# ScalarE's order inside a step of causal attention: copies of turned probabilities before the new tile's exponentials

## The chip, the core and the metric

The program runs on one core of a Trainium2 chip. The metric is the time of one execution on the device, in microseconds, as the median of several runs; lower is better. TensorE (PE) multiplies and transposes, VectorE (DVE) and ScalarE (ACT) read its results out of the eight PSUM banks, GpSimd (POOL) and SyncE (SP) mostly issue DMAs.

## The reference

One inference step of a two-layer trunk: layer 0 mixes tokens by a gated short convolution, layer 1 by multi-head latent attention, and each is followed by a gated convolutional FFN (width 1024, hidden 2816). It is applied to a prompt of 1024 tokens and to 8 sequences with one new token each. The change lies in the prompt's attention:

```python
s = (jnp.einsum('bthc,bsc->bhts', q_lat, kv_lat, preferred_element_type=jnp.float32)
     + jnp.einsum('bthr,bsr->bhts', q_pe, k_pe, preferred_element_type=jnp.float32)) * ATTN_SCALE
mask = k_pos[None, :] <= q_pos[:, None]
s = jnp.where(mask[None, None], s, jnp.finfo(jnp.float32).min)
p = jax.nn.softmax(s, axis=-1).astype(kv_lat.dtype)
return jnp.einsum('bhts,bsc->bthc', p, kv_lat)
```

There are 8 heads. The kernel computes it per head with expanded keys (128 wide, plus 64 rotated) and expanded values (128 wide), which is the same function.

## The kernel before

Each engine has its own instruction stream, written out by hand; semaphores order them. The weights of every layer pass through TensorE in stages (short convolution, FFN 0, the projections of layer 1, the prompt's attention, the attention of the 8 sequences over their paged cache, FFN 1). The prompt's attention takes from about 1520 us to 1766 us of the profiled span and stands between two of these stages.

The attention works on 64 units: 8 heads by 8 tiles of 128 query rows. Unit n belongs to head n // 8, and its tile is `ORD[n % 8]` with `ORD = [7, 0, 6, 1, 5, 2, 4, 3]`, so a large tile and a small one alternate. Tile i attends to i + 1 blocks of 128 keys. A tile of 4 or more has its scores in two PSUM banks (two such pairs exist), a smaller one in bank 4 (there is one). The chain of one unit n is:

1. TensorE, `scores(n)` (L2286 to L2291). A small tile waits for the exponentials of unit n-2 (`e_ready` of n-1), which free bank 4; a large one for those of unit n-4.
2. VectorE, `top(n)` (L1765): the row maxima.
3. ScalarE, `exp(n)` (L1170): exponentials out of PSUM into `p_small` or `p_big`, with row sums.
4. VectorE, `norm(n)` (L1770, L1773): reciprocal and scaling.
5. TensorE, `turn(n)` (L1861, the helper of all transposes): the probabilities are transposed block by block in items of up to four blocks; items alternate between banks 5 and 6, so item a waits until item a-2 has been copied out.
6. ScalarE, `turned_out(n)` (L1181): the copy of each item into `p_t`. From the second head on it also waits until all `values` of the head before are done, since they read `p_t`.
7. TensorE, `values(n)` (L2313): after units 2, 3, 6 and 7 of a head, the product of values and turned probabilities into bank 7 (8, 6, 4 and 2 products for units 2, 6, 7 and 3; the trace counts each twice). It waits for the copies of unit n and until bank 7 is free.
8. ScalarE, `values_out(n)` (L1191): bank 7 into `oh`, from where SyncE's DMAs (L649) carry it to memory.

Steps run over n. In step n TensorE does `scores(n)`, `turn(n-3)`, `values(n-4)`; VectorE does `top(n)`, then `norm(n-1)`; ScalarE does `exp(n)`, `values_out(n-5)`, `turned_out(n-3)` in the kernel before. The program's last four or five steps have no `scores` and no `exp`.

Of the kernel before, what the change touches and what calls it, by code (L numbers as in the profile page):

```python
# [127 lines left out]
def build(nc, ins, outs):  # L128
# [205 lines left out]
    with ExitStack() as ctx:  # L334
        ps = ctx.enter_context(nc.psum_tensor("ps", [P, 8, 512], F32))

        def bank(b):
            return ps[:, b, :]
# [62 lines left out]
        UNITS = H * KT_TOK  # L401
        PV_AFTER = {2: 3, 3: 0, 6: 2, 7: 1}

        def q_tile(n):
            return ORD[n % KT_TOK]

        def turn_items(n):

            return sum(q_tile(u) // 4 + 1 for u in range(n))

        def values_before(n):

            return sum(u % KT_TOK in PV_AFTER for u in range(n))

        def score_ps(n):
            if q_tile(n) >= 4:
                b = 2 * (n // 2 % 2)
                return ps[:, b:b + 2, :].rearrange("p b n -> p (b n)")[:, 0:(q_tile(n) + 1) * P]
            return bank(4)[:, 0:(q_tile(n) + 1) * P]

        def p_sb(n):
            return (p_big if q_tile(n) >= 4 else p_small)[n // 2 % 3]
# [406 lines left out]
        def _(act):  # L829
# [335 lines left out]
            def exp(n):  # L1165
                nk = (q_tile(n) + 1) * P
                act.wait_ge(nm_ready, n + 1)
                if n >= 6:
                    act.wait_ge(p_t_mm, turn_items(n - 5))
                act.activation(p_sb(n)[:, 0:nk], score_ps(n), ACT.Exp, bias=st[:, 0, n % 4:n % 4 + 1],  # L1170
                               accum_out=st[:, 1, n % 4:n % 4 + 1]).then_inc(e_ready, 1)

            def turned_out(n):
                i = q_tile(n)
                if n >= KT_TOK:
                    act.wait_ge(pv_mm, values_before(n // KT_TOK * KT_TOK))
                for item in range(i // 4 + 1):
                    k0, k1 = 4 * item, min(4 * item + 4, i + 1)
                    a = turn_items(n) + item
                    act.wait_ge(p_t_mm, a + 1)  # L1180
                    act.activation(p_t[i // 2][:, k0:k1, (i % 2) * P:(i % 2 + 1) * P],  # L1181
                                   bank(5 + a % 2)[:, 0:(k1 - k0) * P].rearrange("p (k n) -> p k n", n=P),
                                   ACT.Copy).then_inc(p_t_e, 1)

            def values_out(n):
                if n >= 0 and n % KT_TOK in PV_AFTER:
                    j = values_before(n)
                    act.wait_ge(pv_mm, j + 1)
                    if j >= 2:
                        act.wait_ge(head_out[j % 2], 16 * heads_out(j))  # L1190
                    act.activation(oh[j % 2][:], bank(7)[:, 0:256], ACT.Copy).then_inc(pv_e, 1)  # L1191

            for n in range(UNITS + 5):
                if n < UNITS:
                    exp(n)
                values_out(n - 5)
                if 3 <= n < UNITS + 3:
                    turned_out(n - 3)

            act.wait_ge(head_out[0], 48 * H)  # L1200
            act.wait_ge(head_out[1], 48 * H)
# [41 lines left out]
        def _(dve):  # L1243
# [257 lines left out]
            def down22(d, t0):  # L1501
# [46 lines left out]
                if more:  # L1548
                    for m in range(1, KD):
                        add_x(j0 + 2, m, sqx)  # L1550
                    lo_to(i0 + 5)
                    inv_root(q_post(d, 2) + 1)
                    rs_in(q_post(d, 2) + 1)
                    x_stored(d, 2)
                    modulate(j0 + 2, xc, xc, A, B)
                    h_low(j0 + 2, xc, B, range(KD))
                else:
                    for _, n in y_tiles(2):
                        y_out_tile(yt, n)
                        yt += 1  # L1560
# [911 lines left out]
```

## Time and profile before

| | |
|---|---|
| median of 3 runs | 2880.59 us (2876.94 to 2887.14) |
| the profiled execution | 2884.39 us, its span 2882.6 us |
| TensorE, matmuls and transposes | 2691.8 us busy, 93% of the span |
| VectorE | 1199.4 us, 42% |
| ScalarE | 860.0 us, 30% |
| mean granted clock of TensorE | 0.964 |

TensorE is busy nearly all the time, so the stretches in which it isn't are what an order of work can change. One head of the attention, from the first product of its first scores to that of the next head's, lasts about 30.3 us. Within a head the profile can be read step by step with the list above: the line tells the part of the chain, the shape tells the tile.

### The profile page before, as it was taken

Reading aid. Unit: us, or ns where it says so; the run is one execution under the profiler, and the core shown is the slowest. Engines: PE = TensorE matmul, PEld = TensorE weight load, DVE = VectorE, ACT = ScalarE, POOL = GpSimd, SP = SyncE. Lnnn points to the kernel's source line nnn. Section 1 sums busy time; section 2 is a strip of 40 time slices with the busy share of each in tenths; the row PEclk is TensorE's granted clock in tenths of the full one; section 3 lists DMA queues with packets and bytes.
Section 4 is the critical chain, followed back from the end, with each engine's and each line's share of the span. In section 5 each row is a group of like instructions: output and inputs, shape, how many; then the busy total and the mean of one; then the engine's idle time right before and its main releaser. Section 6 shows DMA issues by size and latency. Waiting matters only on the chain.

```text
span 2882.6 us, 39971 instructions
## 1 busy us (share of the span) xinstructions
PE 2691.8 (93%) x17488; PEld 2498.7 (87%) x17488; DVE 1199.4 (42%) x1849; ACT 860.0 (30%) x1359; POOL 123.7 (4%) x183
## 2 busy tenths in 40 slices
PE   5899999899999999997998888987989999999997
PEld 3888999899999999997946666657989999999997
DVE  3522237533333346653443333434743333334553
ACT  3211124222121234432333434423422222214342
POOL 1000000000000000000010000200000000000000
PEclk7999999899999999998999999987989999999998
DMA  9565223121121156542100123624312112116653
GB/s 344 217 233 200 79 99 109 59 66 60 59 72 59 59 185 202 184 134 80 30 16 14 35 110 137 272 95 145 123 52 70 61 59 66 59 61 198 201 169 117
DMA packets 320847, 330.71 MB, mean 115 GB/s; under 512 B 14349, under 2 KB 297330, under 8 KB 310877
## 3 DMA queue, kind: packets, MB, share of 16 engines
q1 hardware_dynamic: 299089, 205.48, 22.8%
q0 software_dynamic: 21584, 122.67, 11.1%
q8 instruction: 138, 2.26, 0.3%
q14 instruction: 36, 0.29, 0.0%
HBM read 282.85 MB, written 45.48 MB: 114 GB/s over the span
## 4 chain that ended last, share of the span: by engine, by line
PE 84%; DVE 8%; DMA 3%; ACT 3%; issue 2%; POOL 0%; DVEq 0%; ACTq 0%; SPq 0%; POOLq 0%
PE ps L1992 15%; PE ps L1994 15%; PE ps L1993 15%; PE ps L2027 7%; PE ps L2029 6%; PE ps L2028 6%; PE ps L1861 4%; PE ps L2313 2%; PE ps L2286 2%; PE ps L1870 1%; DVE ss_x L1343 1%; DVE o_sb L1403 1%; DVE xc L1408 1%; PE ps L1908 1%; PE ps L2377 1%
## 5 line engine op out<-in xcount | busy, mean ns | idle before, releaser
L1992 PE MATMUL ps<-h_hi,w_hi 128*128 128x344 f32 x2832 | 914.6, 323 | 30.3 <-DVE h_lo L1383 30.3
L1993 PE MATMUL ps<-h_lo,w_hi 128*128 128x344 f32 x2832 | 910.0, 321 | 0.0
L1994 PE MATMUL ps<-h_hi,w_lo 128*128 128x344 f32 x2832 | 909.5, 321 | 0.0
L1992 PEld LDWEIGHTS ps<-h_hi,w_hi 128*128 128x128 f32 x2832 | 538.2, 190 | 38.9 <-DVE h_lo L1383 31.1
L1994 PEld LDWEIGHTS ps<-h_hi,w_lo 128*128 128x128 f32 x2832 | 537.4, 190 | 0.0
L1993 PEld LDWEIGHTS ps<-h_lo,w_hi 128*128 128x128 f32 x2832 | 537.0, 190 | 0.0
L1260 DVE TENSOR_TENSOR w_lo<-w_raw,w_hi 128x1024 fp32r<-128x1024 f32 (+1 forms) x278 | 325.5, 1177 | 325.3 <-ACT w_hi L837 324.8
L837 ACT ACTIVATE w_hi<-w_raw 128x1024 fp32r<-128x1024 f32 (+1 forms) x278 | 281.9, 1019 | 414.5 <-DMA w_raw<-in_ffn_w_out 158.6
L2027 PE MATMUL ps<-act_hi,w_hi 128*128 128x344 f32 x832 | 269.3, 324 | 23.8 <-DVE act_lo L1433 17.5
L2029 PE MATMUL ps<-act_hi,w_lo 128*128 128x344 f32 x832 | 268.7, 323 | 0.0
L2028 PE MATMUL ps<-act_lo,w_hi 128*128 128x344 f32 x832 | 268.1, 322 | 0.0
L1590 DVE TENSOR_TENSOR g_sb<-y_sb,ps 128x1032 f32<-128x1032 f32 x52 | 63.9, 1229 | 338.9 <-PE ps L1994 326.6
L2027 PE MATMUL ps<-h_hi,w_hi 128*128 128x344 f32 x608 | 197.2, 324 | 2.1 <-DVE h_lo L1433 1.8
L2029 PE MATMUL ps<-h_hi,w_lo 128*128 128x344 f32 x608 | 194.7, 320 | 0.0
L2028 PE MATMUL ps<-h_lo,w_hi 128*128 128x344 f32 x608 | 194.4, 320 | 0.0
L2027 PEld LDWEIGHTS ps<-act_hi,w_hi 128*128 128x128 f32 x832 | 158.7, 191 | 24.5 <-issue 20.4
L2028 PEld LDWEIGHTS ps<-act_lo,w_hi 128*128 128x128 f32 x832 | 158.5, 190 | 0.0
L2029 PEld LDWEIGHTS ps<-act_hi,w_lo 128*128 128x128 f32 x832 | 158.4, 190 | 0.0
L1033 ACT ACTIVATE a_sb<-ps 128x1032 f32<-128x1032 f32 x52 | 53.7, 1034 | 343.6 <-PE ps L1994 343.6
L1565 DVE COPY tail<-a_sb 128x10 f32<-128x10 f32 x52 | 9.0, 172 | 276.6 <-ACT a_sb L1033 276.6
L2027 PEld LDWEIGHTS ps<-h_hi,w_hi 128*128 128x128 f32 x608 | 114.8, 189 | 2.3 <-issue 2.0
L2029 PEld LDWEIGHTS ps<-h_hi,w_lo 128*128 128x128 f32 x608 | 114.8, 189 | 0.0
(297 smaller groups left out, 2957.4 us busy)
## 6 DMA issues: line engine op xcount, KB each, us to landing
w_raw<-in_ffn_w_out SPq DMA_DIRECT2D x96, 512.0 KB, 4.0
w_raw<-in_ffn_w_in SPq DMA_DIRECT2D x88, 512.0 KB, 3.7
mod_late<-in_mod_w SPq DMA_DIRECT2D x24, 1536.0 KB, 10.2
w_raw<-in_ffn_w_out SPq DMA_DIRECT2D x48, 384.0 KB, 3.4
act_d<-g_sb POOLq DMA_DIRECT2D x52, 344.0 KB, 3.1
xc<-x_d POOLq DMA_DIRECT2D x12, 1376.0 KB, 6.5
x_d<-xc POOLq DMA_DIRECT2D x9, 1376.0 KB, 5.0
mod_raw<-in_mod_w SPq DMA_DIRECT2D x8, 1536.0 KB, 23.6
```

Of the source, the lines that this page charges most:

```text
L837: act.activation(w_hi[k.slot][:, 0:k.kt, :], w_raw[k.slot][:, 0:k.kt, :], ACT.Copy).then_inc(hi_ready, 1)
L1260: dve.tensor_tensor(w_lo[k.slot][:, 0:k.kt, :], w_raw[k.slot][:, 0:k.kt, :], w_hi[k.slot][:, 0:k.kt, :].bitcast(F32), ALU.subtract).then_i ...
L1590: dve.tensor_tensor(chunked(g_sb[f % 2][:]), chunked(y_sb[:]), upset(parity), ALU.mult).then_inc(g_ready, 1)
L1861: return pe.transpose(out, in_, ident[0:r, 0:r])
L1992: pe.matmul(o, w_hi[k.slot][:, t, :], h_hi[:, t, up_cols(c)], start=t == 0, stop=False)
L1993: pe.matmul(o, w_hi[k.slot][:, t, :], h_lo[:, t, up_cols(c)], start=False, stop=False)
L1994: ins = pe.matmul(o, w_lo[k.slot][:, t, :], h_hi[:, t, up_cols(c)], start=False, stop=t == KD - 1)
L2027: pe.matmul(o, w_hi[k.slot][:, t, :], hi[:, t, :], start=k0 + t == 0, stop=False)
L2028: pe.matmul(o, w_hi[k.slot][:, t, :], lo[:, t, :], start=False, stop=False)
L2029: ins = pe.matmul(o, w_lo[k.slot][:, t, :], hi[:, t, :], start=False, stop=k0 + t == parts[-1][1] - 1)
L2286: pe.matmul(o, qno[:, h, rows], kno[:, h, k0:k1], start=True, stop=False)
L2313: ins = pe.matmul(bank(7)[:, c:256], v_sb[:, h, k, :], p_t[g][:, k, c:256], start=k == 0, stop=k >= 2 * g, skip_group_check=True)
```

## The change

In every step ScalarE now does `values_out(n-5)`, then `turned_out(n-3)`, then `exp(n)`. Nothing is added or left out; the orders of TensorE, VectorE, GpSimd and SyncE are the same, and so are all semaphores and buffers.

```diff
             for n in range(UNITS + 5):
-                if n < UNITS:
-                    exp(n)
                 values_out(n - 5)
                 if 3 <= n < UNITS + 3:
                     turned_out(n - 3)
+                if n < UNITS:
+                    exp(n)
```

On ScalarE, this is how the instructions of steps 32 to 34 (the first three of head 4) stand before the change; every head after the first has the same pattern. `p_big` and `p_small` are the outputs of the exponentials, `oh` those of `values_out`, `p_t` those of `turned_out`:

```order
L1170 ACTIVATE p_big_156,st<-ps,st 128x1024 [waits p_t_mm,nm_ready]
L1191 ACTIVATE oh_160<-ps 128x256 [waits head_out1,pv_mm]
L1181 ACTIVATE p_t_152<-ps 128x3x128 [waits p_t_mm,pv_mm]
L1170 ACTIVATE p_small_158,st<-ps,st 128x128 [waits p_t_mm,nm_ready]
L1181 ACTIVATE p_t_153<-ps 128x4x128 [waits p_t_mm,pv_mm]
L1181 ACTIVATE p_t_153<-ps 128x128 [waits p_t_mm]
L1170 ACTIVATE p_big_178,st<-ps,st 128x896 [waits p_t_mm,nm_ready]
L1181 ACTIVATE p_t_152<-ps 128x4x128 [waits p_t_mm,pv_mm]
```

And with the change, the same three steps:

```order
L1191 ACTIVATE oh_160<-ps 128x256 [waits head_out1,pv_mm]
L1181 ACTIVATE p_t_152<-ps 128x3x128 [waits p_t_mm,pv_mm]
L1170 ACTIVATE p_big_156,st<-ps,st 128x1024 [waits p_t_mm,nm_ready]
L1181 ACTIVATE p_t_153<-ps 128x4x128 [waits p_t_mm,pv_mm]
L1181 ACTIVATE p_t_153<-ps 128x128 [waits p_t_mm]
L1170 ACTIVATE p_small_158,st<-ps,st 128x128 [waits p_t_mm,nm_ready]
L1181 ACTIVATE p_t_152<-ps 128x4x128 [waits p_t_mm,pv_mm]
L1170 ACTIVATE p_big_178,st<-ps,st 128x896 [waits p_t_mm,nm_ready]
```

The copy of 3 blocks (unit 29) stood behind the exponentials of 1024 keys (unit 32) and now stands ahead of them; the copies of unit 30, of 4 blocks and of 1, stood behind the exponentials of unit 33 and now stand ahead.

A second place, again on ScalarE, is the turn from one head to the next, steps 35 and 36. Before:

```order
L1170 ACTIVATE p_small_179,st<-ps,st 128x256 [waits p_t_mm,nm_ready]
L1191 ACTIVATE oh_159<-ps 128x256 [waits head_out0,pv_mm]
L1181 ACTIVATE p_t_154<-ps 128x4x128 [waits p_t_mm,pv_mm]
L1181 ACTIVATE p_t_154<-ps 128x4x128 [waits p_t_mm]
L1170 ACTIVATE p_big_155,st<-ps,st 128x768 [waits p_t_mm,nm_ready]
L1191 ACTIVATE oh_160<-ps 128x256 [waits head_out1,pv_mm]
L1181 ACTIVATE p_t_151<-ps 128x128 [waits p_t_mm,pv_mm]
```

With the change:

```order
L1191 ACTIVATE oh_159<-ps 128x256 [waits head_out0,pv_mm]
L1181 ACTIVATE p_t_154<-ps 128x4x128 [waits p_t_mm,pv_mm]
L1181 ACTIVATE p_t_154<-ps 128x4x128 [waits p_t_mm]
L1170 ACTIVATE p_small_179,st<-ps,st 128x256 [waits p_t_mm,nm_ready]
L1191 ACTIVATE oh_160<-ps 128x256 [waits head_out1,pv_mm]
L1181 ACTIVATE p_t_151<-ps 128x128 [waits p_t_mm,pv_mm]
L1170 ACTIVATE p_big_155,st<-ps,st 128x768 [waits p_t_mm,nm_ready]
```

The exponentials of unit 35 (256 keys) stood ahead of `oh` and of the two copies of unit 32, which wait for the products of head 3's last values (`pv_mm`); they now stand behind both. The exponentials of unit 36 (768 keys) stood ahead of the next `oh` and of the copy of unit 33's one block, and now stand behind these.

## Rows read from the trace of the kernel before

The attention's steps are numbered as above; head 4 begins with step 32. Times are microseconds from the span's start.

**Rows 1.** The page's first part: busy time of TensorE over the span

```profile
PE 2691.8 (93%) x17488; PEld 2498.7 (87%) x17488; DVE 1199.4 (42%) x1849; ACT 860.0 (30%) x1359; POOL 123.7 (4%) x183
```

**Rows 2.** Windows, one head each: us, busy of PE, PEld, DVE, ACT, POOL; PEclk, DMA

```profile
1637.07:1667.41 30.34, 25.66 (x133) 19.15 (x133) 10.85 (x24) 12.20 (x32) 5.84 (x6) 1.00 0.49 192
1667.41:1697.78 30.37, 25.69 (x133) 19.18 (x133) 10.79 (x24) 12.20 (x32) 0.00 (x0) 1.00 0.26 103
1697.78:1729.77 31.99, 27.31 (x134) 19.98 (x133) 10.79 (x24) 12.20 (x32) 0.00 (x0) 0.95 0.06 17
```

**Rows 3.** Waits, 1515 to 1770 us (us in total, times, longest)

```profile
PE ps L1861 <- ACT p_t L1181: 20.5, 17, 1.9
...
PE ps L2313 <- ACT oh L1191: 15.2, 16, 1.3
...
PEld ps L2286 <- ACT p_small L1170: 0.3, 1, 0.3
```

**Rows 4.** ScalarE's copies by line, 1515 to 1770 us (busy, mean ns, idle before)

```profile
L1181 ACT ACTIVATE p_t<-ps 128x512 f32<-128x512 f32 (+2 forms) x96 | 43.6, 496 | 14.3 <-PE ps L2313 13.5 <-PE ps L1861 0.7
```

**Rows 5.** Timeline of steps 32 to 34 (start us, us, engine, line; idle before)

```profile
1635.59 1.02 PE L2286 MATMUL ps<-kno,qno 128*128 128x512 f32 x2
...
1638.34 0.49 PE L1861 MATMUL ps<-ident,p_small 128*128 128x128 f32 x3
...
1639.17 0.62 PE L1861 MATMUL ps<-ident,p_big 128*128 128x128 f32 x4
...
1639.80 1.11 ACT L1170 ACTIVATE p_big<-ps,st 128x1024 f32<-128x1024 f32 x1 [4.32 <-DVE st L1765]
...
1641.16 0.49 ACT L1181 ACTIVATE p_t<-ps 128x384 f32<-128x384 f32 x1
...
1641.71 0.33 PE L1861 MATMUL ps<-ident,p_big 128*128 128x128 f32 x1 [1.91 <-ACT p_t L1181]
...
1644.74 2.54 PE L2313 MATMUL ps<-p_t,v_sb 128*128 128x256 f32 x12
```

**Rows 6.** Timeline of step 35

```profile
1648.57 0.47 ACT L1170 ACTIVATE p_small<-ps,st 128x256 f32<-128x256 f32 x1 [1.35 <-DVE st L1765]
...
1649.55 1.75 PE L2313 MATMUL ps<-p_t,v_sb 128*128 128x256 f32 x8 [0.61 <-ACT oh L1191]
```

**Rows 7.** Timeline of steps 36 to 38

```profile
1651.14 1.02 PE L2286 MATMUL ps<-kno,qno 128*128 128x512 f32 x2
1651.34 1.09 ACT L1181 ACTIVATE p_t<-ps 128x512 f32<-128x512 f32 x2 [1.94 <-PE ps L2313]
...
1653.35 0.81 PE L2286 MATMUL ps<-kno,qno 128*128 128x384 f32 x2
...
1655.59 0.28 ACT L1181 ACTIVATE p_t<-ps 128x128 f32<-128x128 f32 x1
...
1655.92 0.55 PE L1861 MATMUL ps<-ident,p_big 128*128 128x128 f32 x3 [0.86 <-ACT p_t L1181]
...
1658.37 3.41 PE L2313 MATMUL ps<-p_t,v_sb 128*128 128x256 f32 x16
```

**Rows 8.** Timeline of step 39

```profile
1663.98 0.69 ACT L1170 ACTIVATE p_small<-ps,st 128x512 f32<-128x512 f32 x1 [3.64 <-DVE st L1765]
...
1664.66 0.37 ACT L1191 ACTIVATE oh<-ps 128x256 f32<-128x256 f32 x1
...
1665.18 0.89 PE L2313 MATMUL ps<-p_t,v_sb 128*128 128x256 f32 x4 [1.30 <-ACT oh L1191]
```

**Rows 9.** Timeline of TensorE in the last steps, without exponentials

```profile
1759.77 0.33 PE L1861 MATMUL ps<-ident,p_big 128*128 128x128 f32 x1 [0.20 <-ACT p_t L1181]
1760.40 0.63 PE L1861 MATMUL ps<-ident,p_small 128*128 128x128 f32 x4 [0.31 <-ACT p_t L1181]
...
1763.97 1.32 PE L2313 MATMUL ps<-p_t,v_sb 128*128 128x256 f32 x5 [0.56 <-ACT oh L1191]
```

**Rows 10.** Timeline of TensorE at step 50

```profile
1702.62 1.92 PE L2286 MATMUL ps<-kno,qno 128*128 128x512 f32 x2
```

## The prediction

> **What bounds the kernel now.** I read the page's first part first: TensorE is busy 2691.8 us of the span, 93% [rows 1], so time can come only from stretches where it isn't, or from its clock. Then windows over the attention, one head each: of 30.34 us TensorE is busy 25.66, VectorE 10.85 and ScalarE 12.20 [rows 2]. ScalarE and VectorE have more than half of each head free; what is missing on TensorE is therefore not their throughput but the moment at which one of their results comes. The list of waits names it: transposes (L1861) wait for the copies of `turned_out` 17 times, 20.5 us in all, and the values' products (L2313) wait for `values_out` 16 times, 15.2 us [rows 3]. TensorE waits for practically no exponential: one weight load of scores, 0.3 us [rows 3].
>
> The timeline of one head says why. In step 33 TensorE has turned four blocks of unit 30 and stands still for 1.91 us before the last one, released by a copy of three blocks that begins at 1641.16 [rows 5]. What that copy needs was done at 1638.34 + 0.49 = 1638.83, and ScalarE was idle for 4.32 us, until 1639.80 [rows 5]. It stood in its stream before the exponentials of unit 32, for VectorE's maxima, with the ready copy behind it. The other three stalls of a head have the same form: 0.61 us in step 35 [rows 6], 0.86 us in step 37 [rows 7], 1.30 us in step 39 [rows 8]. Together 1.91 + 0.61 + 0.86 + 1.30 = 4.68 us per head, and 30.34 - 4.68 = 25.66, TensorE's busy time of a head [rows 2]. These four waits are all that TensorE lacks there.
>
> **The change, part by part.** No instruction is added or removed and none gets another shape, so no duration changes. Only ScalarE's order does, and nothing of its DMAs or of SyncE's and GpSimd's queues is passed by. I take the four places in turn and ask when the awaited copy would end.
>
> Step 33: the copy of unit 29 can start at 1638.83 and takes 0.49, so ends at 1639.32. TensorE wants it at 1641.71 - 1.91 = 1639.80 [rows 5]. It is 0.48 us early; all of the 1.91 goes.
>
> Step 35: the values' products of unit 30 end at 1644.74 + 2.54 = 1647.28 [rows 5]. `values_out` is now the first thing of ScalarE's step and takes 0.37, to 1647.65. TensorE wants it at 1649.55 - 0.61 = 1648.94 [rows 6]. 1.3 us early; the 0.61 goes.
>
> Step 37: here the change adds a wait. The copies of unit 32 wait for the last values of the head before, which end at 1649.55 + 1.75 = 1651.30 [rows 6], and the trace has them start at 1651.34, after 1.94 us of idle time, for 1.09 us [rows 7]. The exponentials of unit 35, which ran at 1648.57 [rows 6], are now queued behind them, with `values_out` of unit 31 and the copy of unit 33 behind those. So: copies to 1652.43, exponentials 0.47 and some 0.1 for reading the accumulator, to 1653.0, `values_out` 0.37 to 1653.4, then unit 33's block, whose turning ends just after TensorE has gone on at 1653.35, and its copy of 0.28 [rows 7]: about 1653.8. TensorE wants that copy at 1655.92 - 0.86 = 1655.06 [rows 7]. 1.2 us early; the 0.86 goes.
>
> Step 39: the values of unit 34 end at 1658.37 + 3.41 = 1661.78 [rows 7]; `values_out` ends at 1662.15. It is wanted at 1665.18 - 1.30 = 1663.88 [rows 8]; the 1.30 goes. The parts of TensorE's stream between these places move together, so the distances hold after the stalls are gone.
>
> What is late now is exponentials. Who waits for them: `scores` of a small tile two units later, and `norm`, whose product is turned three steps later. The worst is unit 35 above: `scores(37)` needs it and starts at 1653.35 [rows 7], against 1653.0. That margin is 0.35 us, the thinnest of all. Elsewhere the exponentials only let pass copies of 0.28 to 1.09 us, and have a step or more in hand: those of unit 39 start at 1663.98 [rows 8] and would start some 0.5 us later, for scores more than 3 us on. I take the cost of the added waits as nothing. The lower bound is nothing as well (no exponential is done earlier than wanted now), the upper: if the margin of 0.35 us is overdrawn by as much again, 7 turns of heads x 0.35 = 2.5 us.
>
> A rule of the Trainium skill speaks against the change here: "TensorE: Matmul & The Clock Gate", in the section on the array's sub-arrays, has ScalarE's queue as strict first in, first out, so a copy that waits for TensorE holds up a ready exponential just as the exponential held up the copies. The 4.32 us of idle time with a ready copy behind [rows 5] bears that out. By the rule alone every head would have such a hold-up, and it is the one worked out for unit 35; the sum doesn't change by it.
>
> The last steps have no exponentials, so their stalls stay: 0.20 and 0.31 us for copies, 0.56 us for `values_out` [rows 9]. The sum over the attention: (20.5 - 0.20 - 0.31) + (15.2 - 0.56) = 19.99 + 14.64 = 34.6 us. Against the profiled execution, 2884.39 us, that is 2849.8 us. That execution lies 3.8 us above the median of the runs shown, so from the median: 2880.59 - 34.6 = **2846.0 us**. Behind the attention everything starts by semaphores of its end, so the gain isn't given back there.
>
> **The rivals.**
>
> The clock gives some more. At step 50 TensorE's products take 1.92 us for two where they take 1.02 at step 36 [rows 10, 7], and that head lasts 31.99 us at a mean clock of 0.95, against 30.37 us at 1.00 for the one before [rows 2]: 1.2 instead of 2.4 GHz for a while, around a 1.91 us stall of the kind that goes away. Without it 1.6 us more are saved: 2844.4 us. For it: the stall lies in that stretch; against: six other heads have the same stall and keep the clock. The Trainium skill, "TensorE: Matmul & The Clock Gate", Part 1, has the clock throttled after idle time and released by activity; by that fewer gaps can only help. It fits this head, not the six others.
>
> Only part of the stalls goes. If the products still wait for something else at the time that `values_out` used to release them (the copies of the same unit, from the same engine), only the 20.0 us of transposes are saved: 2860.6 us. If it is the transposes that stay, only 14.6: 2866.0 us. For it: both waits hang on one engine. Against: every margin above is 0.48 us or more.
>
> It does nothing measurable. This would be so if TensorE's stalls were only handed on, from a copy to `norm` on VectorE, say, which comes behind a later exponential: 2880.6 us. Against: VectorE is busy 10.85 of 30.34 us [rows 2], and `turn` comes three steps after `scores`.
>
> It gets slower. The mechanism: the exponentials gate TensorE after all, because a small tile's scores need the exponentials of two units earlier and these now stand behind copies that themselves wait for TensorE: a closed ring, in which every copy lengthens the step. Its price is all copies, 43.6 us [rows 4], so 2880.6 + 43.6 - 34.6 = 2889.6 us. It decides from the point at which copies and exponentials take longer than TensorE's way to the next small scores: at step 36 they take 1.09 + 0.57 = 1.66 us against 1653.35 - 1651.30 = 2.05 us [rows 7], and everywhere else TensorE's way is longer.
>
> **How the numbers follow.** The full saving: 0.80, within it 0.50 at 2846.0 and 0.30 with the clock's 1.6 us. Part of it: 0.10. Nothing: 0.05. Slower: 0.05. The range starts at 2844.4 less the 3.7 us by which the fastest run shown lies under the median, about 2840, and reaches up over 2846.0 + 2.5 + 6.5 (the slowest run's distance) = 2855 to the nearer of the partial cases, 2861. A measurement of this kernel tells about 0.3%, 8.6 us, from no change. Faster by more than that: 0.80 + 0.10 = 0.90; within it 0.05; slower 0.05.
>
> **What the profile after would show.** Right: the waits of L1861 for L1181 and of L2313 for L1191 shrink from 20.5 and 15.2 us to about 0.5 each, in the last steps; a head's window is about 25.7 us with TensorE busy all of it; ScalarE's idle time before L1181 and L1191, with TensorE as releaser, rises, and that before the exponentials falls. Wrong: TensorE waiting in L2286 for L1170 (the ring), or in L1861 for VectorE's L1773 (the stall handed on), or a head that lasts 27 to 29 us. A clock below 1.00 in the attention's middle would take back part of it, and so would a later stage that takes longer than before though its instructions are the same.

## The result, and the profile after

| | before | after |
|---|---|---|
| median | 2879.65 us (6 runs, 2876.94 to 2887.14) | 2835.98 us (6 runs, 2834.42 to 2837.96) |
| the profiled execution, its span | 2884.39, 2882.6 us | 2835.91, 2834.1 us |
| the attention: first scores to the first product of L2384 | 1519.73 to 1768.40: 248.7 us | 1519.26 to 1725.50: 206.2 us |
| behind it | 1114.2 us | 1108.6 us |

The ratio of the times is 0.9843 (95%: 0.9832 to 0.9855): 43.7 us less, where 34.6 were forecast. The direction and the mechanism were right, the size was not, and the time lies below the range.

The page's first part of after, as [rows 1]:

```profile
PE 2679.9 (95%) x17488; PEld 2495.1 (88%) x17488; DVE 1199.2 (42%) x1849; ACT 864.0 (30%) x1359; POOL 124.1 (4%) x183
```

TensorE's busy time fell by 11.9 us although it executes the same 17488 instructions. That is the first hint at what the prediction missed (the kernel before measured again had 2688.9 us, so some 3 of the 11.9 us are scatter). Windows of after over the heads that [rows 2] show for before, from the values' products of unit 2 of one head to those of the next (us, busy of PE, PEld, DVE, ACT and POOL, PEclk, DMA):

```profile
1635.08:1659.85 24.77, 24.77 (x134) 19.14 (x133) 10.78 (x25) 12.66 (x32) 1.88 (x2) 1.00 0.72 295
1659.85:1684.57 24.72, 24.72 (x135) 19.14 (x133) 10.79 (x25) 12.77 (x32) 0.00 (x0) 1.00 0.08 22
```

A head takes 24.7 us, not the 25.66 of the forecast, and TensorE is busy in all of it. Its busy time per head fell as well, from 25.66 to 24.77 us. The waits of after, 1515 to 1740 us, as [rows 3]:

```profile
ACT p_t L1181 <- PE ps L1861: 43.3, 38, 2.2
...
ACT oh L1191 <- PE ps L2313: 21.7, 17, 1.9
ACT p_t L1181 <- PE ps L2313: 19.5, 7, 2.8
...
PE ps L1861 <- ACT p_t L1181: 0.8, 2, 0.6
...
PEld ps L2286 <- ACT p_small L1170: 0.6, 2, 0.3
...
PE ps L2313 <- ACT oh L1191: 0.6, 1, 0.6
```

TensorE's stalls are gone but for the last steps. (The two weight loads of scores that wait for an exponential, 0.6 us in all, are in head 0, at 1527.80 and 1532.00 us; before had one of them.) ScalarE now waits for TensorE's transposes and values; in before the copies waited 13.5 us for values and 0.7 us for transposes [rows 4]. The timeline of steps 32 to 35, as [rows 5, 6]:

```profile
1619.09 0.49 PE L1861 MATMUL ps<-ident,p_small 128*128 128x128 f32 x3
...
1619.68 0.49 ACT L1181 ACTIVATE p_t<-ps 128x384 f32<-128x384 f32 x1 [2.14 <-PE ps L1861]
...
1619.92 0.73 PE L1861 MATMUL ps<-ident,p_big 128*128 128x128 f32 x5
...
1620.55 1.12 ACT L1170 ACTIVATE p_big<-ps,st 128x1024 f32<-128x1024 f32 x1 [0.38 <-PE ps L1861]
...
1623.36 2.54 PE L2313 MATMUL ps<-p_t,v_sb 128*128 128x256 f32 x12
...
1625.95 0.38 ACT L1191 ACTIVATE oh<-ps 128x256 f32<-128x256 f32 x1 [0.59 <-PE ps L2313]
...
1627.40 1.68 PE L2313 MATMUL ps<-p_t,v_sb 128*128 128x256 f32 x8
```

The copy of unit 29 starts 0.10 us after its transposes' end, and the five transposes of unit 30 follow each other without a pause; in before the fifth stood apart, at 1641.71 [rows 5]. `values_out` of unit 30 ends 1.1 us before the values of unit 31 begin. Steps 36 and 37, as [rows 7]:

```profile
1628.92 1.02 PE L2286 MATMUL ps<-kno,qno 128*128 128x512 f32 x2
1629.12 1.09 ACT L1181 ACTIVATE p_t<-ps 128x512 f32<-128x512 f32 x2 [2.79 <-PE ps L2313]
...
1630.09 0.48 ACT L1170 ACTIVATE p_small<-ps,st 128x256 f32<-128x256 f32 x1
...
1630.45 0.21 ACT L1170 ACTIVATION_READ_ACCUMULATOR p_small<-ps,st 128x1 f32 x1
...
1630.54 0.40 ACT L1191 ACTIVATE oh<-ps 128x256 f32<-128x256 f32 x1
...
1631.14 0.81 PE L2286 MATMUL ps<-kno,qno 128*128 128x384 f32 x2
...
1631.39 0.28 ACT L1181 ACTIVATE p_t<-ps 128x128 f32<-128x128 f32 x1 [0.46 <-PE ps L1861]
```

Here is the hold-up of the exponentials: the copies wait for the values of unit 31, and the exponentials of unit 35 end with their accumulator's reading at 1630.66, 0.48 us before `scores(37)` at 1631.14. The forecast had 0.35 us. The values' products of units 34 and 35, as [rows 7, 8]; their starts are 5.33 us apart, 6.81 in before:

```profile
1635.08 3.41 PE L2313 MATMUL ps<-p_t,v_sb 128*128 128x256 f32 x16
...
1640.41 0.82 PE L2313 MATMUL ps<-p_t,v_sb 128*128 128x256 f32 x4
```

### The profile page after: what moved, and what is told of

The parts are those of the page before. It is cut to its first block, busy times and chain, and to the rows that moved or that the text cites. A ratio compares the mean times of both kernels' runs of the same rounds, so it can differ in the third digit from the quotient of the medians.

```text
span 2834.1 us, 39971 instructions
## 1 busy us (share of the span) xinstructions
PE 2679.9 (95%) x17488; PEld 2495.1 (88%) x17488; DVE 1199.2 (42%) x1849; ACT 864.0 (30%) x1359; POOL 124.1 (4%) x183
## 4 chain that ended last, share of the span: by engine, by line
PE 85%; DVE 8%; DMA 3%; ACT 2%; issue 1%; POOL 0%; DVEq 0%; SPq 0%; ACTq 0%; POOLq 0%
PE ps L1992 16%; PE ps L1994 15%; PE ps L1993 15%; PE ps L2027 6%; PE ps L2029 6%; PE ps L2028 6%; PE ps L1861 4%; PE ps L2313 2%; PE ps L2286 2%; PE ps L1870 1%; DVE ss_x L1343 1%; DVE o_sb L1403 1%; DVE xc L1408 1%; PE ps L1908 1%; PE ps L2354 1%
## 5 line engine op out<-in xcount | busy, mean ns | idle before, releaser
L1992 PE MATMUL ps<-h_hi,w_hi 128*128 128x344 f32 x2832 | 914.1, 323 | 30.3 <-DVE h_lo L1383 30.3
```

The source lines that it names most:

```text
L1992: pe.matmul(o, w_hi[k.slot][:, t, :], h_hi[:, t, up_cols(c)], start=t == 0, stop=False)
```

## The experiments

The first experiments ask where the gain beyond the forecast comes from: from the stalls themselves (theory A of the first expectation) or from elsewhere (rival B). Times of each are compared with the kernel before on the same chip (medians 2881.81, 2881.71 and 2879.08 us in the three sets). "Attention" is the stretch of the table above in the run's trace, "head" the distance between the values' products of unit 2 of two heads in the middle.

| run | median, us | ratio (95%) | attention | head |
|---|---|---|---|---|
| values_out alone ahead | 2857.00 | 0.9916 (0.9901 to 0.9932) | 226.1 | 27.4 |
| turned_out alone ahead | 2861.74 | 0.9933 (0.9918 to 0.9948) | 228.0 | 27.7 |
| new order in heads 4 to 7 | 2857.67 | 0.9919 (0.9906 to 0.9933) | 225.0 | 30.34, then 24.7 |
| before again | 2884.9 (one run) | | 248.5 | 30.35; head 6: 31.93 |
| new order in heads 0 to 3 | 2864.94 | 0.9940 (0.9924 to 0.9955) | 231.4 | 24.76, then 30.36; head 6: 31.98 |
| 8 copies for 2 | 2838.21 | 0.9850 (0.9835 to 0.9866) | 205.9 | 24.8 |
| exponentials before the hold | 2837.91 | 0.9850 (0.9836 to 0.9865) | 206.1 | 24.7 |
| zeros early | 2839.73 | 0.9854 (0.9839 to 0.9869) | 204.8 | 24.7 |
| 16 copies for 2 | 2843.09 | 0.9877 (0.9861 to 0.9894) | 210.0 | 25.3 |
| 32 copies for 2 | 2851.11 (one run) | | 216.5 | 26.3 |
| after again | 2836.80 | 0.9852 (0.9835 to 0.9868) | 206.3 | 24.7 |
| zeros early, again | 2838.33 | 0.9857 (0.9841 to 0.9874) | 204.8 | 24.7 |

**Half of the change: values_out.** Against the kernel before:

```diff
             for n in range(UNITS + 5):
-                if n < UNITS:
-                    exp(n)
                 values_out(n - 5)
+                if n < UNITS:
+                    exp(n)
                 if 3 <= n < UNITS + 3:
                     turned_out(n - 3)
```

> Of the change only values_out goes ahead of the exponentials; the copies of turned_out stay behind them. Theory A (a stall costs TensorE more than the idle time that the profile puts before the released instruction, because the last instruction before the pause is shown at its full latency; true cost by starts to starts 0.84 us at step 35's place and 1.55 us at step 39's, 2.13 and 1.09 us for the copies): both values stalls go, the copies come 0.26 us earlier since values_out no longer stands between exponentials and copy, so 7 x 0.84 + 8 x 1.55 + 14 x 0.26 = 21.9 us less than before, a head of about 27.7 us. Rival B (the idle column is the whole cost, and the 8 us that the change saved beyond it came from elsewhere, the clock or later stages): 14.6 + 3.6 = 18.2 us less, a head of 28.0 us or more. Waits of L1861 for L1181 stay at about 1.65 and 0.60 us a head in both.

Window of one head and waits in this run:

```profile
1649.32:1676.76 27.44, 25.22 (x134) 19.12 (x133) 10.79 (x25) 12.42 (x32) 1.16 (x2) 1.00 0.62 255
```

```profile
PE ps L1861 <- ACT p_t L1181: 17.5, 18, 1.6
...
PE ps L2313 <- ACT oh L1191: 0.6, 1, 0.6
```

The heads are at 27.4 us, 2.9 us under 30.3. The terms of theory A give 0.84 + 1.55 + 2 x 0.26 = 2.91 us per head, those of B 0.61 + 1.30 + 0.52 = 2.43. (The head lengths in the expectation spread the sum over eight heads, but head 0 lacks half of the stalls; the terms per head are what can be compared.) The attention is 22.6 us shorter, of which 1.6 are the clock's, told below: 21.0 us, where A had 21.9 and B 18.2.

**The other half: turned_out.** In the steps 8h+3 the old order must stay: `turned_out` of the next head's first unit waits for the last values, those wait for bank 7, and that for a `values_out` that would stand behind.

```diff
             for n in range(UNITS + 5):
+                early = n % KT_TOK != 3
+                if early and 3 <= n < UNITS + 3:
+                    turned_out(n - 3)
                 if n < UNITS:
                     exp(n)
                 values_out(n - 5)
-                if 3 <= n < UNITS + 3:
+                if not early and 3 <= n < UNITS + 3:
                     turned_out(n - 3)
```

> Of the change only turned_out goes ahead of the exponentials, values_out stays behind them; in the steps 8h+3 the old order stays, because there turned_out waits for values that wait for values_out. Theory A: the copies' stalls go at their cost from start to start, 7 x 2.13 + 8 x 1.09 = 23.6 us; values_out of step 39's place comes about 0.5 us later than before, since its exponentials now stand behind two copies, 8 x 0.5 = 4 us more; sum 19.6 us less than before. Rival B (idle column): 20.0 - 4.0 = 16.0 us less. In both L1861 no longer waits for L1181 and L2313 waits for L1191 about 1.8 and 0.6 us a head.

The window of one head, and the waits:

```profile
1649.20:1676.90 27.70, 25.26 (x135) 19.20 (x133) 10.79 (x25) 12.66 (x32) 1.87 (x2) 1.00 0.64 262
```

```profile
PE ps L2316 <- ACT oh L1191: 19.5, 16, 1.8
...
PE ps L1864 <- ACT p_t L1181: 0.7, 2, 0.5
```

L2313's wait (L2316 here) is 1.8 us at its longest, as expected: the exponentials of step 39 are now late by two copies. A head gives 30.35 - 27.70 = 2.65 us; A's terms 2.13 + 1.09 - 0.5 = 2.72, B's 1.91 + 0.86 - 0.5 = 2.27. The halves give 2.9 and 2.7, the whole 5.6. They add up, because two side effects nearly cancel: 0.52 us more in the first half, 0.5 us less in the second.

**Half of the heads.** The new order from head 4 on, and in another kernel the new order up to head 3 (the two conditions exchanged). The first, against after:

```diff
-                if n < UNITS:
+                if n < UNITS and n < UNITS // 2:
                     exp(n)
                 values_out(n - 5)
                 if 3 <= n < UNITS + 3:
                     turned_out(n - 3)
+                if UNITS // 2 <= n < UNITS:
+                    exp(n)
```

> The old order in heads 0 to 3, the new one in heads 4 to 7. Theory A: a head costs 30.3 us in the old order and 24.7 in the new one, so 4 x 5.6 = 22.4 us less than before, and about 21 us more than the change. Rival B (the heads give 4.68 us each and the rest of the change's gain lies outside the heads): 18.7 us less than before, with heads 4 to 7 at 25.7 us. A third reading: the lapse of the clock at step 50 of the kernel before cost 1.6 us and is gone in both.

One trace with both orders, a head of each:

```profile
1600.83:1631.17 30.34, 25.65 (x135) 19.16 (x133) 10.79 (x25) 12.22 (x32) 0.00 (x0) 1.00 0.06 18
1682.22:1706.94 24.72, 24.72 (x135) 19.14 (x134) 10.78 (x25) 12.77 (x32) 0.00 (x0) 1.00 0.08 22
```

The same engine, program and clock, 5.62 us apart: 4.69 us of idle time (30.34 - 25.65) and 0.93 us of TensorE's "busy" time. This is where B falls.

> The new order in heads 0 to 3, the old one in heads 4 to 7. By starts to starts again 4 x 5.6 = 22.4 us less than before; by the idle column 18.7 us. It also asks what the half-speed stretch in head 6 hangs on: two traces of the kernel before have it at the same place, the three partial kernels don't. If it comes from the old order's stalls, one of the heads 4 to 7 has it here (a head of about 32 us); if it hangs on where the whole sequence lies in time, it may be gone, since heads 4 to 7 begin 20 us earlier.

```profile
1642.49:1672.85 30.36, 25.68 (x135) 19.18 (x134) 10.86 (x25) 12.20 (x32) 0.94 (x1) 1.00 0.55 225
1672.85:1704.83 31.98, 27.30 (x135) 19.98 (x134) 10.78 (x25) 12.20 (x32) 0.00 (x0) 0.95 0.06 17
```

The attention is 17.2 us shorter than in before again and the median 16.8, not 22.4. The expectation counted head 0 as a whole head; it has few stalls (nothing to turn yet in its steps 1 and 3). From values to values three heads gain 5.6 us each; where the orders change, the kernel with the other half shows 26.27 us, 4.1 gained, so 1.5 are left for this one; head 0 gives 0.5. That is 18.8 us. The half-speed stretch in head 6 is there again, though that head starts some 16 us earlier, and this trace has another one in head 4. TensorE's timeline there:

```profile
1624.19 0.33 PE L1863 MATMUL ps<-ident,p_big 128*128 128x128 f32 x1 [1.92 <-ACT p_t L1181]
1624.35 1.15 PE L2288 MATMUL ps<-kno,qno 128*128 128x512 f32 x2
...
1626.15 1.48 PE L2288 MATMUL ps<-kno,qno 128*128 128x384 f32 x2
```

The two products of 512 columns after the 1.92 us stall take 1.15 us, those of 384 columns 1.48 us, where after has 1.02 and 0.81 for such pairs. The granted clock there:

```profile
1626.00:1628.00 2.00, 2.00 (x6) 1.11 (x6) 0.00 (x0) 0.00 (x0) 0.00 (x0) 0.50 0.00 0
```

That is 1.2 GHz. With 1.6 us for this second lapse 17.2 us are left, as measured.

**The kernel before, again.**

> The kernel before, unchanged, for a second trace. If the half-speed stretch at 1700 us (a head of 31.99 us instead of 30.37) belongs to the kernel, it is there again and is part of what the change took away; if it is chance, all eight heads last 30.3 to 30.4 us here. The attention, from the first product of scores to the first of L2384, was 248.7 us: expected 247 to 249. What lies behind the attention took 4.6 us longer in the profiled execution of before than in that of after; if that is scatter of the executions, it is smaller here.

```profile
1690.09:1722.02 31.93, 27.24 (x134) 19.99 (x133) 10.78 (x25) 12.22 (x32) 0.00 (x0) 0.95 0.06 17
```

Head 6 is long again, with a mean clock of 0.95. What lies behind the attention took 1113.4 us, close to the 1114.2 of the first trace of before, though the expectation had less if the difference to after was scatter.

**How much the exponentials can be held up.** Each of the two copies of four blocks of tile 7 in one-block copies, then in halves and quarters of blocks. The core of the edit, against after (eight copies):

```diff
-                    act.activation(p_t[i // 2][:, k0:k1, (i % 2) * P:(i % 2 + 1) * P],
-                                   bank(5 + a % 2)[:, 0:(k1 - k0) * P].rearrange("p (k n) -> p k n", n=P),
-                                   ACT.Copy).then_inc(p_t_e, 1)
+                    parts = range(k0, k1) if i == 7 and n >= KT_TOK else (k0,)
+                    width = 1 if i == 7 and n >= KT_TOK else k1 - k0
+                    for k in parts:
+                        ins = act.activation(p_t[i // 2][:, k:k + width, (i % 2) * P:(i % 2 + 1) * P],
+                                             bank(5 + a % 2)[:, (k - k0) * P:(k - k0 + width) * P].rearrange("p (k n) -> p k n", n=P),
+                                             ACT.Copy)
+                    ins.then_inc(p_t_e, 1)
```

> The change, and the two copies of four blocks of every head's largest tile (q tile 7, from the second head on) split into eight copies of one block. In the trace of after these two take 1.09 us together, then the exponentials of unit 8h+3 run until 1630.66, and TensorE begins scores(8h+5) at 1631.14: a margin of 0.48 us. One copy of one block takes 0.28 us alone, so eight take 1.6 to 2.3 us: 0.5 to 1.2 us more. The slower rival's ring decides exactly here: from 0.48 us of delay on, every further 0.1 us is a stall in all 7 heads, so 0 to 7 x (0.7 + 0.2) = 6 us more than after, and the waits show L2286 for L1170 seven times. If exponentials do not gate TensorE at all, it is the same as after and L2286 waits for nothing.

Timeline of step 35 to 37 with eight copies:

```profile
1629.63 1.47 ACT L1184 ACTIVATE p_t<-ps 128x128 f32<-128x128 f32 x8 [2.79 <-PE ps L2317]
...
1631.27 0.27 ACT L1170 ACTIVATION_READ_ACCUMULATOR p_small<-ps,st 128x1 f32 x1
...
1631.65 0.85 PE L2290 MATMUL ps<-kno,qno 128*128 128x384 f32 x2
```

Eight copies took 1.47 us, less than the 1.6 to 2.3 expected; the exponentials ended at 1631.54, 0.11 us before the scores. Nothing was lost, which says only that the dose was too small.

> As the run with eight copies, but every block in two halves: 16 copies for the two of four blocks. With eight, the copies took 1.47 us in a stream instead of 1.09 and the exponentials' end was still 0.11 us ahead of scores(8h+5); nothing was lost. By those two durations a copy of 64 columns takes about 0.12 us in a stream, so 16 take 2.0 us, and the exponentials end 0.4 us too late: with 0.2 us for the drain and restart of TensorE, 0.6 us a head, 7 x 0.6 = 4 us more than after, heads of 25.3 to 25.4 us instead of 24.75, and L2286's line waits for L1170 in all 7 heads. If exponentials don't gate TensorE, heads stay at 24.75.

The timeline, the window of one head and the wait with 16 copies:

```profile
1629.38 1.97 ACT L1186 ACTIVATE p_t<-ps 128x64 f32<-128x64 f32 x16 [2.79 <-PE ps L2319]
...
1631.42 0.37 ACT L1170 ACTIVATION_READ_ACCUMULATOR p_small<-ps,st 128x1 f32 x1
...
1631.84 0.91 PE L2292 MATMUL ps<-kno,qno 128*128 128x384 f32 x2 [0.28 <-ACT p_small L1170]
```

```profile
1661.21:1686.49 25.28, 24.99 (x135) 19.17 (x133) 10.79 (x25) 13.65 (x46) 0.00 (x0) 1.00 0.07 22
```

```profile
PE ps L2292 <- ACT p_small L1170: 2.0, 7, 0.3
```

TensorE stood idle for 0.28 us per head, and a head grew from 24.74 to 25.28 us, by 0.54. The difference, 0.26, is in its busy time, now 24.99 us. Against after again the attention is 3.7 us longer, as the heads say, and the median 6.3, where 4 was expected; the rest lies behind the attention (1111.5 against 1107.6 us).

> The same with 32 copies of 32 columns: some 3.0 us for them, the exponentials end about 1.4 us too late, 1.6 us a head with drain and restart: heads of about 26.4 us, 11 us more than after. If the loss per head doesn't grow by as much as the copies do from 16 to 32, something else than the ring of copies, exponentials and scores is at work.

```profile
1670.50:1696.80 26.30, 25.00 (x134) 19.18 (x133) 10.88 (x25) 14.52 (x62) 0.00 (x0) 1.00 0.07 21
```

```profile
PE ps L2292 <- ACT p_small L1170: 9.1, 7, 1.3
```

1.3 us idle per head, 1.56 us lost, busy 25.00 us. From 16 to 32 copies the idle time grew by 1.0 us a head and the head by 1.0 us; the 0.26 stayed. So the ring of copies, exponentials and scores exists and binds once the margin that the trace shows is used up (not at eight copies, 0.11 us short of it, but at 16), and a stall has a price beside its idle time that didn't grow with it.

**No hold-up.** Against after:

```diff
             for n in range(UNITS + 5):
+                held = n >= KT_TOK and n % KT_TOK == 3
                 values_out(n - 5)
+                if held and n < UNITS:
+                    exp(n)
                 if 3 <= n < UNITS + 3:
                     turned_out(n - 3)
-                if n < UNITS:
+                if not held and n < UNITS:
                     exp(n)
```

> The change, but in the steps 8h+3 of the later heads the exponentials stand behind values_out and ahead of the two copies that have to wait for the last values of the head before. If the hold-up of the exponentials costs nothing, as the margin of 0.48 us says, this is the same as after within 1 us; if it costs something that the waits don't show, it is faster by up to 7 x 0.5 us. The idle time of ScalarE before its copies stays.

ScalarE in steps 35 and 36 of this run:

```profile
1629.63 0.47 ACT L1170 ACTIVATE p_small<-ps,st 128x256 f32<-128x256 f32 x1 [0.86 <-DVE st L1768]
1630.00 0.19 ACT L1170 ACTIVATION_READ_ACCUMULATOR p_small<-ps,st 128x1 f32 x1
1631.56 1.09 ACT L1181 ACTIVATE p_t<-ps 128x512 f32<-128x512 f32 x2 [1.37 <-PE ps L2316]
```

The exponentials end 1.4 us before the copies start, and the heads still last 24.7 us. The hold-up inside the margin is free.

**A shorter way out of the attention.** VectorE's zeros for the next stage, against after:

```diff
             dve.wait_ge(p_t_e, turn_items(UNITS))
-            dve.wait_ge(pv_e, 4 * H)
             step(dve.memset(ps[:, 4:6, :], 0.0))
-            step(dve.memset(bank(7), 0.0))
             step(dve.memset(w_pad[:], 0.0))
             step(dve.tensor_reduce(sel[:], ident[:].rearrange("p (g w) -> p w g", w=32)[:, 0:H, :], AX.X, ALU.add))
+            dve.wait_ge(pv_e, 4 * H)
+            step(dve.memset(bank(7), 0.0))
```

> The change, and behind the attention VectorE's zeroing of banks 4 and 5 (0.91 us), of w_pad (0.17) and the reduction to sel (0.12) stand ahead of its wait for the last values_out, only the zeroing of bank 7 (0.48 us) behind it. TensorE stands 2.7 us there in the trace of after, from 1722.82 to 1725.50. Expected: 1.2 to 1.5 us less than after, and, if the half-speed stretch that after has from 1723.1 us comes from that pause, up to 3 us more. Rival: the pages' turning that follows waits for something else, and nothing changes.

> The changed kernel, unchanged, on the same chip as the others of this call: heads of 24.7 to 24.8 us, the attention 206 us, the time 2834 to 2839 us. What lies behind the attention was 1108.6 us in its first trace and 1106.8 to 1114.2 us in the others, a scatter that goes with how long the clock is at half speed there; expected within that again.

> VectorE's zeroing of banks 4 and 5 ahead of the wait for the last values_out, a second time, now beside after on the same chip. In its first trace the attention was 204.8 us instead of 206.2, but the median was no lower than that of the neighbouring variants. If the 1.4 us reach the end, it is 1.4 us less than after here; if the scatter of the clock behind the attention swallows it, no difference can be told.

The end of the attention in after, and then with the zeros early:

```profile
1722.86 0.38 ACT L1191 ACTIVATE oh<-ps 128x256 f32<-128x256 f32 x1 [1.94 <-PE ps L2313]
...
1723.63 0.91 DVE L1785 MEMSET ps<- 128x1024 f32 x1 [6.70 <-ACT oh L1191]
...
1725.50 0.38 PE L2384 MATMUL ps<-qlat,lats 128*8 128x64 f32 x4 [2.67 <-issue]
```

```profile
1724.20 0.38 ACT L1191 ACTIVATE oh<-ps 128x256 f32<-128x256 f32 x1 [1.94 <-PE ps L2313]
1724.76 0.48 DVE L1788 MEMSET ps<- 128x512 f32 x1 [3.13 <-ACT oh L1191]
...
1725.45 0.38 PE L2384 MATMUL ps<-qlat,lats 128*8 128x64 f32 x4 [1.29 <-DVEq L1790]
```

From the last `values_out` to TensorE it is 1.25 us instead of 2.64, and the attention is 1.4 to 1.5 us shorter in both traces. The medians don't show it: 2838.33 us against 2836.80 for after on the same chip, with runs that overlap (2835.71 to 2839.84 and 2834.39 to 2838.96). Behind the attention this variant took 1109.6 and 1110.2 us, after 1108.6 and 1107.6. The other part of the expectation came too: the stretch at 1.2 GHz that follows the attention is shorter, with a mean granted clock of 0.83 from 1725 to 1735 us where after has 0.66. What lies behind became longer even so. At the products of L2377 150 us behind the attention's end, this variant is still 0.2 us ahead of after; at the next stage's first turning (tile `top_n`), 17 us on, it is 1.0 us behind, in both pairs of traces, and between the two the granted clock is lower (0.57 against 0.79 in the 8 us from 158 us behind the attention's end). So the clock goes with that loss; why it falls sooner there stays open. No version here beats the changed kernel.

## Why the prediction was wrong

**What was right.** The diagnosis: four stalls per head, all of ready copies behind exponentials that waited for VectorE. All four went, in full, and those of the last steps stayed (0.8 and 0.6 us; 0.5 and 0.56 were forecast). The instructions kept their durations: the sum of ScalarE's records in the attention is 119 us in both, though its busy time per head rose from 12.20 to 12.7 us because fewer of them overlap. The margins at steps 33, 35, 37 and 39 were 0.4, 1.1, 1.2 and 1.4 us (0.48, 1.3, 1.2 and 1.7 by the forecast's figures, which let a copy start the moment its input was done, where the trace has 0.1 to 0.2 us between them). The one added wait, `scores(37)` for unit 35, costs nothing, which the doses confirm. The partial, the null and the slower rival didn't come; the slower one's ring is real, and was 0.48 us away.

**The step that failed** is the sum of the stalls, "4.68 us per head" and "34.6 us": a mis-sized term. It took the idle time before the released instruction as the price of a stall, and seemed confirmed by 30.34 - 4.68 = 25.66, "TensorE's busy time", as though that were a floor. Both come from the same records, in which the instruction before a pause and the first after it carry time that in a stream lies under their neighbours. The rows on record could have told: in [rows 5] three transposes take 0.49 us and four 0.62, so one more in the stream adds 0.13, while the one behind the pause takes 0.33, 0.20 more. After confirms it: from the first transposes of unit 30 to the first values of unit 30 it was 1644.74 - 1639.17 = 5.57 us in [rows 5], and is 1623.36 - 1619.92 = 3.44 us, 2.13 less, where the idle column says 1.91. With the same reading the other places give 0.84, 1.08 and 1.56 (idle column 0.61, 0.86 and 1.30): 5.61 us per head, and 0.22 to 0.26 us per stall beyond its idle time. TensorE's busy time per head counts the stalls:

| stalls in a head | run | busy, us |
|---|---|---|
| 0 | after | 24.72 to 24.77 |
| 1 | 16 or 32 copies | 24.99, 25.00 |
| 2 | either half of the change | 25.22, 25.26 |
| 4 | before | 25.66 |

By this count it is 0.23 to 0.27 us per stall. Seven heads from values to values gain 7 x 5.6 = 39.2 us, the rest of head 0 0.5 and the last steps 1.1: 40.8 us, where the prediction had 34.6. The 10.0 us between the forecast 2846.0 and the measured 2835.98 are then these 6.2, 1.6 of the clock (next), 0.9 by which the median of before is lower with six runs than with the three shown, and 1.3 outside the attention. What inside TensorE makes up the quarter of a microsecond no run here shows; that it is paid, and once per stall, they do.

**The clock.** The prediction gave 0.30 to a head 6 that loses its 1.6 us and kept them out of its number. All three traces with the old order in head 6 have the stretch at 1.2 GHz there (32.0, 31.93 and 31.98 us for the head), and none of the others, with new or partly new order, has it. It comes right behind that head's stall of 1.91 us (step 49; the slow products of [rows 10] are the next ones), and the additional one, with the new order in heads 0 to 3, behind the same stall of head 4 (step 33). So it goes with the old order's longest stall and not with a moment in time; the stalls of 1.84 us that `turned_out` alone ahead has in its heads, and those of 1.64 us with `values_out` alone ahead, have no such stretch behind them. With it, the attention is 42.4 us shorter (248.7 to 206.2). Why the other heads with the same stalls kept 2.4 GHz stays open.

**The rest.** 43.7 us in the medians are 42.4 in the attention and about 1 elsewhere, which is less than the runs of one kernel differ. In the profiled executions behind the attention 5.6 us are missing too, but that stretch took 1106.8 to 1111.5 us in all changed kernels' traces and 1114.2 and 1113.4 in the two of before, and the medians don't have it. Added up from the granted clocks of windows of 8 us (an estimate), TensorE was at 1.2 GHz for some 87 and 86 us of it in the two traces of before, 80 and 72 in the two of after, and up to 87 in the other changed kernels; so the clock's scatter can be a part of the 5.6 us. Whether a part belongs to the change wasn't settled.

## What to carry to other kernels

Price a stall of TensorE by starts: from the start of an instruction well before the pause to the start of one behind it, less what the same pair takes where nothing waits. The idle column leaves out a quarter of a microsecond per stall here, and the busy time of the engine is no floor, since it contains it; with four stalls a head that was a sixth of the gain (0.93 of 5.61 us).

In an engine that serves two chains in order, put what is ready first and the work that waits for a third engine last, and look for the one place where the new order waits instead. Its margin can be read before the change is built (0.35 us forecast, 0.48 found), and an experiment with longer copies shows how far it reaches.

## What was not expected of the hardware

Stalls cost TensorE 0.22 to 0.27 us beside their idle time, whether they last 0.28 or 1.9 us. The clock fell to 1.2 GHz behind a stall of 1.91 us at the same step of the program in three traces of two kernels, and not behind most of the other stalls of that length. ScalarE's small copies in a stream cost less than alone: eight of 128 columns took 1.47 us, 0.18 each, and 16 of 64 columns 1.97 us, 0.12 each, where one of 128 alone takes 0.28. The same data in two copies of 512 columns took 1.09 us.
